# The last layer norm of a two-block transformer kernel: means from single-column products on TensorE, turned blocks read in PSUM, and VectorE's order rewritten

## The reference

```python
def _layer_norm(x, g, b):
    xf = x.astype(jnp.float32)
    mu = jnp.mean(xf, axis=-1, keepdims=True)
    var = jnp.mean(jnp.square(xf - mu), axis=-1, keepdims=True)
    return ((xf - mu) * lax.rsqrt(var + LN_EPS) * g + b).astype(x.dtype)

...
        h = x * (1.0 + scale2) + shift2
        y = _conv_ffn(h, w_up[l], conv_w[l], conv_b[l], w_down[l])
        x = _layer_norm(DEEPNORM_ALPHA * x + gate2 * y, ln2_g[l], ln2_b[l])
```

## Time and profile before

| | |
|---|---|
| median of 3 runs | 1812.11 us (1811.92 to 1812.45) |
| profiled execution, own time | 1814.47 us |
| its span, first to last instruction | 1812.7 us |
| TensorE busy | 1765.8 us, 97% |
| VectorE busy | 972.2 us, 54% |
| ACT busy | 674.5 us, 37% |
| GpSimd busy | 825.2 us, 46% |
| mean granted TensorE clock | 0.989 of full speed |

### The profile page before, as it was taken

One profiled execution on the slowest core, in us unless ns is written; L12 is line 12 of the kernel. 1 busy time (PEld: TensorE's weight loads), 2 busy tenths in 40 slices (PEclk: granted clock), 3 DMA queues, 4 the chain that ended last, 5 costly groups with the idle time before them and its releaser, 6 DMA issues. The chain is left out here.

```text
span 1812.7 us, 26173 instructions
## 1 busy us (share of the span) xinstructions
PE 1765.8 (97%) x8981; PEld 1496.2 (83%) x8981; DVE 972.2 (54%) x1608; ACT 674.5 (37%) x1390; POOL 825.2 (46%) x664
## 2 busy tenths in 40 slices
PE   7999999999999999999999999899999899999996
PEld 5888888888777888888888888699988878888886
DVE  4257535668965477152125367466567673552545
ACT  4322222243476433232233233655532552332332
POOL 3553454567970455444545455100034465455450
PEclk9999999999999999999999999999999999999998
DMA  6454452533311345433333333100012134323321
GB/s 203 126 164 151 140 152 81 174 99 111 94 43 40 121 148 188 136 91 107 100 89 107 103 95 93 47 2 1 1 58 83 47 99 134 101 85 105 95 79 47
DMA packets 279700, 178.49 MB, mean 98 GB/s; under 512 B 6264, under 2 KB 258356, under 8 KB 279476
## 3 DMA queue, kind: packets, MB, share of 16 engines
q1 hardware_dynamic: 265348, 149.35, 28.3%
q10 hardware_dynamic: 14256, 27.87, 4.4%
HBM read 175.11 MB, written 2.10 MB: 98 GB/s over the span
## 5 line engine op out<-in xcount | busy, mean ns | idle before, releaser
L630 POOL TENSOR_TENSOR wL<-raw,wH 128x512 fp32r<-128x512 f32 (+2 forms) x560 | 747.6, 1358 | 916.7 <-ACT wH L1358 915.4
L731 PE MATMUL ps<-actH,wH 128*128 128x512 f32 (+1 forms) x1312 | 511.8, 390 | 8.1 <-DVE actL L2254 4.4
L731 PE MATMUL ps<-actH,wL 128*128 128x512 f32 (+1 forms) x1312 | 506.0, 386 | 0.0
L731 PE MATMUL ps<-actL,wH 128*128 128x512 f32 (+1 forms) x1312 | 506.0, 386 | 0.0
L1358 ACT ACTIVATE wH<-raw 128x512 fp32r<-128x512 f32 (+2 forms) x560 | 312.7, 608 | 339.6 <-PE ps L731 337.7
L731 PEld LDWEIGHTS ps<-actH,wH 128*128 128x128 f32 x1312 | 248.3, 189 | 58.8 <-issue 4.5
L731 PEld LDWEIGHTS ps<-actH,wL 128*128 128x128 f32 x1312 | 248.3, 189 | 49.6
L731 PEld LDWEIGHTS ps<-actL,wH 128*128 128x128 f32 x1312 | 248.2, 189 | 49.3 <-issue 0.7
L731 PE MATMUL ps<-hidH,wH 128*128 128x512 f32 (+1 forms) x720 | 267.6, 372 | 0.0
L731 PE MATMUL ps<-hidH,wL 128*128 128x512 f32 (+1 forms) x720 | 266.6, 370 | 0.0
L731 PE MATMUL ps<-hidL,wH 128*128 128x512 f32 (+1 forms) x720 | 266.5, 370 | 0.0
(11 more groups left out here) (320 smaller groups left out, 2037.6 us busy)
## 6 DMA issues: line engine op xcount, KB each, us to landing
mod_raw<-in_w_mod ACTq DMA_DIRECT2D x24, 1024.0 KB, 5.8
raw<-in_w_in SPq DMA_DIRECT2D x48, 512.0 KB, 3.7
raw<-in_ffn_w_gate SPq DMA_DIRECT2D x44, 512.0 KB, 3.9
raw<-in_ffn_w_up SPq DMA_DIRECT2D x44, 512.0 KB, 3.8
raw<-in_w_up SPq DMA_DIRECT2D x44, 512.0 KB, 3.8
raw<-in_ffn_w_down SPq DMA_DIRECT2D x32, 512.0 KB, 3.8
raw<-in_w_out SPq DMA_DIRECT2D x16, 512.0 KB, 3.7
raw<-in_w_down SPq DMA_DIRECT2D x16, 512.0 KB, 3.6
```

The costliest lines, as they stand in the source:

```text
L630: nc.gpsimd.tensor_tensor(wL[:, b:b + w // 2], raw[:, b:b + w // 2], wH[:, b:b + w // 2].bitcast(F32), ALU.subtract).then_inc(lo_ready, 1)
L731: return nc.tensor.matmul(out, a, b, start=first, stop=last)
```

## The change

On TensorE the mean of each token comes from products of x with one column of `ones` (which holds 1/1024). For a token block and a feature tile, x's 128x128 piece is the weights and the column the moving operand; the product is that tile's share of the mean, one number per token. `mean_columns(pair, b, ks)` does this for two token blocks and the feature tiles ks, into columns of bank b; one VectorE reduce over 8 columns per block gives the mean. The turned blocks of the second feature half are no longer copied: ACT's square and VectorE's gained block read them in PSUM. The columns and transposes of the first pair move into half 1's slot 0, behind k = 3 of 8; for the second pair most stand behind slot 2 and the rest behind the last slab. The hook is therefore called for every k. VectorE's list is rewritten.

```diff
+        def mean_columns(pair, b, ks):
+
+            for q in (2 * pair, 2 * pair + 1):
+                for k in ks:
+                    mm = product(ps[:, b, (q % 2) * KT + k:][:, 0:1], x[:, k * S + q * P:][:, 0:P], ones[:, 0:1], True, True)
+            if KT - 1 in ks:
+                mm.then_inc(fin_cols, 1)
...
-            def hook(half, j):
-                if half == 0 and j in (1, 2):
+            def hook(half, j, k):
+                if half == 0 and j in (1, 2) and k == K - 1:
+                    pe.wait_ge(drained_v, d0 + 4)
                     for q in (2 * j - 2, 2 * j - 1):
-                        natural(q, range(4), lambda k: (drained_v, d0 + k + 1))
-                if half == 1 and j == 1:
+                        natural(q)
+                if (half, j, k) == (1, 0, 3):
+                    pe.wait_ge(fin_sum, ST)
+                    pe.wait_ge(half_drained, 2 * 4)
+                    mean_columns(0, 6, range(KT))
                     for q in range(2):
-                        pe.wait_ge(fin_sum, q + 1)
-                        natural(ST + q, range(4), lambda k: (half_drained, 4 + k + 1))
+                        natural(ST + q)
+                if (half, j, k) == (1, 2, K - 1):
+                    pe.wait_ge(fin_centre, 1)
+                    pe.wait_ge(drained_v, d0 + 6)
+                    mean_columns(1, 0, range(6))
+                    for q in range(2, ST):
+                        natural(ST + q, (0, 1))
...
-            for q in range(2, ST):
-                pe.wait_ge(fin_sum, q + 1)
-                natural(ST + q, range(4), lambda k: (drained_v, d0 + 4 + k + 1))
+            for k in (2, 3):
+                pe.wait_ge(drained_v, d0 + 4 + k + 1)
+                for q in range(2, ST):
+                    natural(ST + q, (k,))
+                mean_columns(1, 0, (4 + k,))
...
             if n >= ST:
-                act.wait_ge(fin_copy, q + 1)
+                act.wait_ge(fin_T, n + 1)
...
-            nc.scalar.activation(tile(sq2, n % 2), out_block(n), ACT.Square, scale=D ** -0.5, bias=ssq[:, 8 + q:9 + q],
+            nc.scalar.activation(tile(sq2, n % 2), bank(4 + q) if n >= ST else out_block(n), ACT.Square, scale=D ** -0.5, bias=ssq[:, 8 + q:9 + q],
...
+        def final_mean(pair, b):
+
+            two = slice(2 * pair, 2 * pair + 2)
+            dve.wait_ge(fin_cols, pair + 1)
+            V.tensor_reduce(mean[:, two], bank(b, 2 * KT).rearrange("p (q k) -> p q k", q=2), AX_X, ALU.add).then_inc(fin_centre, 1)
+            dve.wait_ge(fin_centre, pair + 1)
+            link(V.tensor_tensor(md[:, two], mean[:, two], c_neg[:, two], ALU.add))
...
+            V.scalar_tensor_tensor(out_block(n), bank(4 + q) if half else out_block(n), mean[:, q:q + 1],
+                                   ln2_gB[:, half * 512:half * 512 + 512], ALU.subtract, ALU.mult)
...
-        for j in range(SLOTS):
+        for j in range(3):
             half_tile("f3_down2", 0, j, 40, 4)
         dve.wait_ge(fin_sum, ST)
         link(V.tensor_scalar(c_neg, total, -2.0 / D, None, ALU.mult))
-        link(V.tensor_scalar(c_half, total, -1.0 / D, None, ALU.mult))
         V.tensor_scalar(c_bias, total, -2.0 * D ** -1.5, None, ALU.mult).then_inc(fin_mean, 1)
-        for j in range(2):
-            half_tile("f3_down2", 1, j, 40, 4)
+        half_tile("f3_down2", 0, 3, 40, 4)
+        half_tile("f3_down2", 1, 0, 40, 4)
         dve.wait_ge(gb_in, 32)
-        final_mean(0)
-        for half in range(2):
-            gained_block(0, half)
+        final_mean(0, 6)
+        gained_block(0, 0)
+        gained_block(1, 0)
+        gained_block(0, 1)
+        half_tile("f3_down2", 1, 1, 40, 4)
+        gained_block(1, 1)
         final_rn(0)
         half_tile("f3_down2", 1, 2, 40, 4)
-        for half in range(2):
-            last_block(0, half)
+        last_block(0, 0)
+        last_block(0, 1)
         half_tile("f3_down2", 1, 3, 40, 4)
-        final_mean(2)
-        for half, q in ((0, 1), (1, 1), (0, 2), (0, 3), (1, 2), (1, 3)):
-            gained_block(q, half)
-        final_rn(2)
-        for q in range(1, ST):
+        last_block(1, 0)
+        last_block(1, 1)
+        final_mean(1, 0)
+        gained_block(2, 0)
+        gained_block(3, 0)
+        gained_block(2, 1)
+        gained_block(3, 1)
+        final_rn(1)
+        for q in range(2, ST):
```

More of the change, by code:

```diff
@@ L395, in _build @@
     conv_c, conv_act = sem("conv_c"), sem("conv_act")
-    fin_T, fin_sum, fin_mean, fin_sq, fin_copy = (sem(n) for n in (
-        "fin_T", "fin_sum", "fin_mean", "fin_sq", "fin_copy"))
+    fin_T, fin_sum, fin_mean, fin_sq, fin_cols, fin_centre = (sem(n) for n in (
+        "fin_T", "fin_sum", "fin_mean", "fin_sq", "fin_cols", "fin_centre"))
     half_done, half_drained = sem("half_done"), sem("half_drained")
@@ L867, in first_slabs, with natural @@
                     then()
-        def natural(n, tiles, ready):
+        def natural(n, ks=range(4)):
             half, q = n // ST, n % ST
-            for k in range(4):
-                pe.wait_ge(*ready(k))
+            for k in ks:
                 mm = nc.tensor.transpose(bank(4 + q, P, k * P), x[:, (4 * half + k) * S + q * P:][:, 0:P], ident)
-            mm.then_inc(fin_T, 1)
+            if 3 in ks:
+                mm.then_inc(fin_T, 1)
+        def mean_columns(pair, b, ks):
+            for q in (2 * pair, 2 * pair + 1):
+                for k in ks:
+                    mm = product(ps[:, b, (q % 2) * KT + k:][:, 0:1], x[:, k * S + q * P:][:, 0:P], ones[:, 0:1], True, True)
+            if KT - 1 in ks:
+                mm.then_inc(fin_cols, 1)
         def token_halves(name, ready, K, seen, early, hook):
@@ L901, in token_halves @@
                                            half_of(hidH, k, half), half_of(hidL, k, half), k == 0, k == K - 1)
[L902 to L903 removed]
+                        if k == K - 1:
+                            mm.then_inc(slab_done if half else half_done, 1)
+                        hook(half, j, k)
         def last_down(ready, K):
             d0 = drain_base["f3_down2"]
[L909 to L910 removed]
+            def hook(half, j, k):
+                if half == 0 and j in (1, 2) and k == K - 1:
+                    pe.wait_ge(drained_v, d0 + 4)
                     for q in (2 * j - 2, 2 * j - 1):
[L912 to L921 removed]
+                        natural(q)
[3 more added lines that the diff above has]
+                    mean_columns(0, 6, range(KT))
+                    for q in range(2):
+                        natural(ST + q)
[5 more added lines that the diff above has]
+                        natural(ST + q, (0, 1))
+            token_halves("f3_down2", ready, K, 4, lambda j, k: None, hook)
+            for k in (2, 3):
[3 more added lines that the diff above has]
+                mean_columns(1, 0, (4 + k,))
         def third_slabs():
@@ L1327, in _ @@
         token_halves("out2", (hid_ready, 2 * (NF + KT) - KT), KT, 0, provisional_mean,
-                     lambda half, j: moments(0) if (half, j) == (1, 0) else spread_moments(0) if (half, j) == (1, 2) else None)
+                     lambda half, j, k: None if k < KT - 1 or half == 0 else
+                     moments(0) if j == 0 else spread_moments(0) if j == 2 else None)
         up_down("f3", 2 * (NF + KT), None)
@@ L2347, in _ @@
             gated_tile("f3_down2", 0, j, 40)
[L2349 to L2363, removed]
@@ L2365, in gained_block @@
-        def gained_block(q, half):
[L2367 to L2373, removed]
+        total, c_bias, c_neg, mean = ssq[:, 0:ST], ssq[:, 8:8 + ST], ssq[:, 12:12 + ST], ssq[:, 16:16 + ST]
+        md, m2, squares, var = ssq[:, 24:24 + ST], ssq[:, 28:28 + ST], (ssq[:, 32:32 + ST], ssq[:, 36:36 + ST]), small[:, 0:ST]
@@ new lines, in final_mean @@
+        def final_mean(pair, b):
[4 more added lines that the diff above has]
+            link(V.tensor_tensor(md[:, two], mean[:, two], c_neg[:, two], ALU.add))
+        def gained_block(q, half):
+            n = half * ST + q
+            dve.wait_ge(fin_sq, n + 1)
+            V.scalar_tensor_tensor(out_block(n), bank(4 + q) if half else out_block(n), mean[:, q:q + 1],
+                                   ln2_gB[:, half * 512:half * 512 + 512], ALU.subtract, ALU.mult)
@@ L2374, in final_rn @@
+        def final_rn(pair):
+            two = slice(2 * pair, 2 * pair + 2)
             link(V.tensor_tensor(m2[:, two], md[:, two], md[:, two], ALU.mult))
-            dve.wait_ge(fin_sq, ST + q0 + 2)
+            dve.wait_ge(fin_sq, ST + 2 * pair + 2)
             link(V.scalar_tensor_tensor(var[:, two], squares[0][:, two], LN_EPS, squares[1][:, two], ALU.add, ALU.add))
```

## The result

The change makes the kernel slower: 1817.74 us, the median of 18 runs (1815.59 to 1819.1), against 1812.47 (1811.5 to 1814.52) for the kernel before in 18 runs; the ratio is 1.0025, 95% interval 1.0018 to 1.0032. That is 5.3 us more, and the interval lies wholly above 1: the change is slower by about 0.25%. The forecast was 1810.8.

What follows compares the result with a forecast made beforehand. The last half tile, h(1,3), was to change from bound by VectorE to waiting for TensorE: +1.86 us before it and -3.17 behind it, -1.31 in all, set against 1812.11 for 1810.8 us; 8-in-10 range 1809.2 to 1812.8.

Steps and rivals of the forecast that it cites:

- the price of a column product: On TensorE, each added one-column product was taken at 0.101 us, from eight in a row in the middle norm.
- 28 x 0.101: TensorE ahead of slab j=3's end: the added columns' part of the 3.31 us by which that slab would end later.
- rival B: Granted clock falls in slabs j=0 to 2: 1813.7 us; again over slab j=3: 1815.9; chance 0.06, both falls 0.02.
- What bounds the kernel: Last 40 us: VectorE reaches h(1,3), the last half tile of x, late; after the change it waits 1.9 us for TensorE.
- VectorE's walk: VectorE up to h(1,3): h(1,0) at 1788.23, h(1,1) at 1791.11, h(1,3) ready at 1798.56, 1.86 us lost.
- The tail behind h(1,3): VectorE's work from h(1,3) to its end: 13.43 us before, 10.26 after, a gain of 3.17.
- The operations that no row of before showed: On VectorE: the reduce on PSUM taken at 0.20 us, a gained block reading PSUM at nothing extra, within 0.01.
- Rival A: The added columns on TensorE are hidden and cost nothing; h(1,3) bound by VectorE, gain 3.2 us: 1808.9 us; chance 0.07.
- Rival D: Columns on TensorE cost 0.25 us each, unpipelined, 4.2 us later: 1815.0 us, slower; chance 0.02.
- E: VectorE would wait at h(1,1) or h(1,2), too; half a microsecond absorbed at h(1,3); no time or chance of its own.
- Rival C: TensorE's switches cost 0.2 us each, or columns 0.14; TensorE 1.1 us later, gain 0.2: 1811.9 us; chance 0.15.

Runs made afterwards that it cites:

- turns: The changed kernel with two 128x128 transposes in place of each column product, the mean left out: 1814.84 us, ratio to before 1.0010.
- w128: The changed kernel with 128 columns of ones instead of one in each column product: 1814.99 us, ratio to before 1.0010.
- nocols: The changed kernel with one column product left in each group, means not formed, their correction set to zero: 1809.16 us, ratio to before 0.9977.
- spread: The changed kernel with its single-column products dealt out, two at a time between slab products: 1815.6 us, ratio to before 1.0015.
- before_cols: The kernel before with unused column products added, 16 behind half 1 slot 0 and 12 behind slot 2: 1821.48 us, ratio to before 1.0038.
- halfwide: The changed kernel with columns for feature tiles 4 to 7 alone, 128 wide, the other sums from ACT: 1810.89 us, ratio to before 0.9990.

## Why the prediction was wrong

**The step that failed first: the price of a column product.** The prediction read the earlier trace rows as "eight of the same shape" and took 0.101 us for each. The eight records there are four products: the loop in `provisional_mean` runs over four token blocks (line 1306). A float32 product is two records, so the rows gave 0.20 a product, and 0.225 is what the changed kernel shows. The term "28 x 0.101" (2.83 us) should have been about 6.2. The row prints the line of the helper (731), so only its operands, `ones` and `acc`, lead to that loop; counting the products that the code issues there would have settled it. The Trainium skill ("FP8 and Floating Point Precision", TensorE Precision Notes) says that true float32 takes four passes through the array. The trace shows two records for each such product; how the passes lie in them no run here shows.

**The step that failed second: rival B.** It was written out with the right event and the right places, and given 0.06, of it 0.02 for both falls. Both came in both profiles of the changed kernel. The sizes (2.9 and 2.2 us) were too large: the falls cost 1.52 and 1.49, 3.0 us together, for each ended after some three microseconds and not after the 6.6 of the earlier trace rows. That B's time with both falls, 1815.9, comes nearer to the 1817.74 than the forecast is partly luck: it has the falls too dear and the products too cheap. The argument against it was the row of transposes that held 1.00. That row spoke for transposes, which turns confirms, and not for products of one column. I let a row on one kind of instruction answer for another; the changed kernel and turns, side by side, show that the two differ.

Step by step, from h(0,3) to h(1,3):

| stretch of TensorE's time, us | forecast | measured |
|---|---|---|
| 16 products | 1.62 | 3.60 |
| 12 products | 1.21 | 2.60 |
| clock: eight transposes (1787.20 to 1788.80) | 0.79 | 1.60 |
| clock: the seven steps to 1790.43 | 0.92 | 1.63 |
| clock: slab j=3 (1799.77 to 1804.10) | 2.84 | 4.33 |

The differences are 1.98 + 1.39 = 3.37 for the price and 0.81 + 0.71 + 1.49 = 3.01 for the clock, 6.38 in all; the miss was 8.21 - 1.86 = 6.35. The 3.01 agrees with the 2.99 by which w128 is shorter. Had the price alone been off, the result would have been 1810.8 + 3.4 = 1814.2, still within 0.2% of before and outside the range given; the falls of the clock took it past that, and the 1817.74 measured is 0.5 above the 1817.2 that both together give.

**What held.**
- What bounds the kernel: a tail that waits for TensorE in place of one that waits for VectorE, and the start of h(1,3) as the clock that counts. nocols shows it: there the wait is still 0.75 us.
- VectorE's walk: from h(1,0) to h(1,1) and h(1,2) forecast 2.88 and 6.69 us, measured 2.88 and 6.68.
- The tail behind h(1,3): 10.26 forecast and measured, no wait in it.
- The operations that no row of before showed: the reduce of 128x16 in PSUM took 0.17 (0.20 with the step forecast); a pair of gained blocks took 1.40 us reading PSUM and 1.42 reading SBUF; ACT's square took 0.69 from PSUM. So nothing was lost on these reads, and the 0.13 us, an estimate, that the errata section of "VectorE: DVE Perf Modes" in the Trainium skill would have given for them is not there.
- Rival A is out, too: leaving the products away saved 0.227 us for each (nocols), and dealt out they cost the same (spread). Its time was off as well: without the 2.83 us of the products the prediction's own walk puts h(1,3) at 1798.56 - 2.83 = 1795.73, still set by TensorE, a gain of 4.1 us and not 3.2; in nocols, with two products left, TensorE sets it. Rival D had the size of a product (0.25) almost right, for another reason (one record's length without overlap, not two records), so its nearness is luck; the prediction put it at 0.02 and said that "Rows 4 speak against it plainly". E is out: the walk held.
- Rival C: the switches were 0.08 as before (1799.77 to 1799.97 is 0.20, 0.08 above the usual 0.12); its other half, "0.14 a column", failed as the forecast did.

The range given reached to 1812.8 and missed by 4.9 us. Its upper end came from rows of before as they were read, with no room for the reading itself.

**Left open.** What lets the clock fall behind one row of single columns and not behind another was not settled: the first row of before_cols held 1.00, the first row of the changed kernel did not, and between them lie other neighbours (transposes behind it or not) and other places. spread shows that shorter groups kept it at 1.00 in the one execution profiled. Each kernel but the changed one has one profile, so how often a fall comes in it isn't known. Whether columns in float32r would leave one record, and cost half, was not tried.

## What to carry to other kernels

Before a row of a trace is used as a price, hold its count against the code: how many instructions does the line issue, and how many records does the trace show? A float32 product with one column cost as much as one with 128, so on an engine that is the bound a sum over partitions by 28 such products (6.2 us here) should be weighed against one by an engine that stands idle (0.5 us by ACT). And if a row of narrow products must stand on TensorE, make them 128 wide or deal them out: either kept the granted clock at 1.00 in the profile here, and the wide ones saved 3.0 us at the same price. Wide products fill their neighbours' columns, so each must be issued ahead of the one whose column it covers, as in halfwide.

## What the runs showed of the hardware

- The granted clock fell to 0.50 with TensorE busy 3.00 of 3.00 us: behind or within rows of float32 products with one column (3.0 us lost in the changed kernel), in part with 32 columns (0.60 from 1787 to 1790), and not with 128 columns at the same pace, nor in 40 transposes in a row. One row of 32 records with one column (before_cols, from 1785.29) was followed by 1.00.
- A float32 product with 128x128 weights shows as two records of 0.11 us each, whether it has 1, 32 or 128 columns (3.60, 3.54 and 3.57 us for 32 records). A 128x128 transpose is one record of 0.11.
